# Two jobs per loop body over 18 weight slots, with jobs of 96 tokens, in the expert loop of a decoder layer

## The chip, the core and the metric

The kernel runs on one NeuronCore of one Trainium2 chip. The time is the device time of one execution in microseconds. In this text TensorE is PE in the rows, VectorE is DVE, ScalarE is ACT, GpSimd is POOL, and SyncE is SP; PEld is TensorE's weight load.

## The reference

One decoder layer over 512 tokens of width 1024, all in float32: an attention and pooling mixer, then a mixture of 32 experts of which each token takes four, then a last RMSNorm. The change touches the experts alone:

```python
def moe(h, router_w, router_b, w_gate_up, b_gate_up, w_down, b_down):
    logits = (h @ router_w + router_b).astype(jnp.float32)
    top_v, top_i = lax.top_k(logits, TOP_K)          # 4 of 32
    gates = jax.nn.softmax(top_v, axis=-1)
    ...
    def expert_block(args):
        xblk, e = args
        act = clamped_swiglu(xblk @ w_gate_up[e] + b_gate_up[e])
        return act @ w_down[e] + b_down[e]
```

An expert has 1024 x 2048 weights for gate and up and 1024 x 1024 for down, 12.6 MB together. 512 x 4 = 2048 (token, expert) pairs are spread over 32 experts, 64 each in the mean.

## The kernel before

The mixer and the router fill about the first 300 us. Then comes the expert loop, in jobs. A job is one expert with up to 128 of its tokens, cut into chunks of 32 (CH); it has as many chunks as its tokens need, and two at least (LEAST). An expert with more tokens than a job takes would get a second job. The job table (expert, first token, chunks, chunks before, gathered rows) is worked out by VectorE with one matmul (L625) and read by every engine into registers, once a job. With every expert in one job there are 32 jobs.

The weights of a job are 12 units of 1 MB: units 0 to 7 are gate and up (one for each 128 rows of the input), units 8 to 11 are down. The loop uses 12 of the 18 slots of 8 KB per partition that `ring` spans; slots 12 to 17 lie in memory that the mixer and the router use before. SyncE issues all weight loads in one queue, in order: for unit u of the next job it waits until TensorE has read the same unit of this one (`wait_read`), then issues. Unit 7 is released by `gu_done`, unit 11 by `dn_done`, the others by `units_used`, which the last chunk, chunk 0, counts up.

TensorE holds a chunk's 32 tokens as its weights and streams the expert's weights past it, four column tiles side by side. In a job it goes through units 0 to 3 with all chunks in turn, highest chunk first, then through units 4 to 7 for one chunk after another, then through the downs, one chunk after another. A chunk's down waits for its own activation (`act_done`), which VectorE and ScalarE work out (`swiglu`, `sigmoid`) in the order of the chunks while TensorE works on the next. There are code variants for four, three and two chunks:

```python
with pe.If(chunks > 2):
    with pe.If(chunks > 3):
        gates_together((3, 2, 1, 0))
        gate_rest(3)
    with pe.Else():
        gates_together((2, 1, 0))
    gate_rest(2)
with pe.Else():
    gates_together((1, 0))
```

Ahead of its gates, a job first does 16 small matmuls (`indices(job + 1)`, L619) that give the row indices of the next job's tokens. They wait for `hot_done` (VectorE, `job_columns`, L1090, late in the job before). VectorE copies the result (`job_rows`), GpSimd gathers the next job's rows with indirect DMAs (L920), VectorE flips them (`flip_x`, L1169, `x_done`). After a chunk's down VectorE adds the bias (`add_bias`, L1217, `y_done`) and GpSimd scatters the result (L941). The last scatter is followed by the combine: y_rows are read back (L377), summed with the router's gates (L1275), normed, and written.

Of the kernel before, what the change touches and what calls it, by code (L numbers as in the profile page):

```python
# [28 lines left out]
P = 128  # L29
# [23 lines left out]
NCH = P // CH  # L53
# [3 lines left out]
SLOTS = 12  # L57
# [10 lines left out]
JOBS_MAX = 49  # L68
# [16 lines left out]
C_END = C_AFTER + 49  # L85
# [12 lines left out]
def constants():  # L98
# [18 lines left out]
    n = np.arange(C_END - C_AFTER)[None, :]  # L117
    c[:, C_AFTER:C_END] = 16.0 * ((p[:, None] >= 1) & (p[:, None] <= n))
# [14 lines left out]
def program(nc, x, w_in, w_out, norm1, norm2, final_g, rel_bias, pool_w, pool_scale, router_w,  # L133
# [7 lines left out]
    with ExitStack() as ctx:  # L141
# [36 lines left out]
        job_r, job_p, keep_s = st[:, 44:48], st[:, 48:52], st[:, 52:56]  # L178
# [33 lines left out]
        jdiag = work[:, o + 1296:o + 1296 + ROWS * JOBS_MAX]  # L212
        jobs_f = sb("jobs_f", [P, ROWS, JOBS_MAX])
        jobs_i = sb("jobs_i", [P, ROWS, JOBS_MAX], I32)
        njobs_i = sb("njobs_i", [P, 1], I32)
# [9 lines left out]
        hot = work[:, 10240:11264].bitcast(F16).rearrange("p (t n) -> p t n", t=TT)  # L225
        slot = work[:, 11264:11520].bitcast(F16)
        pcol = work[:, 11520:11528].bitcast(F16)[:, 0:3 * TT].rearrange("p (t n) -> p t n", t=TT)
        idx_t = work[:, 11536:11544].rearrange("p (c n) -> p c n", c=NCH)
        idx_g = work[:, 11552:11556].bitcast(U32)
        idx_s = work[:, 11560:11564].bitcast(U32)  # L230
# [78 lines left out]
        def _(sp):  # L309
# [21 lines left out]
            def wait_read(job, u, low):  # L331
# [8 lines left out]
            def load_unit(e, u):  # L340
# [46 lines left out]
        def _(pe):  # L387
# [240 lines left out]
            def run_job(job, chunks, before_job, low):  # L628
# [56 lines left out]
                with pe.Else():  # L685
                    gates_together((1, 0))
# [651 lines left out]
```

## Time and profile before

| | |
|---|---|
| median of 3 runs | 1361.63 us (1360.19 to 1365.3) |
| the profiled execution | 1361.84 us, its span 1360.1 us |
| TensorE busy | 87% of the span, mean granted clock 0.938 |
| VectorE, ScalarE, GpSimd busy | 37%, 13%, 18% |
| DMA | 454.87 MB, 334 GB/s in the mean |
| chain that ended last | PE 67%, DMA 25%, VectorE 3%, issue 3% |

Times of events are in us from the start of the span. A profile row has a line number of the kernel before. "x192" counts records; a float32 matmul leaves two records, and its weight load two more. The idle time in brackets stands before the instruction, with what ended it. "issue" is a wait for nothing that the profile shows.

### The profile page before, as it was taken

What the parts mean: (1) busy time and instruction counts of PE and PEld (TensorE: products, weight loads), DVE (VectorE), ACT (ScalarE), POOL (GpSimd) and SP (SyncE); (2) the same over time, 40 slices, a digit from 0 to 9 for tenths busy, and PEclk for the clock granted to TensorE, in tenths of its full rate; (3) what the DMA queues carried; (4) which work ended last, traced back from release to release, by engine and by line L of the source; (5) the groups of instructions that cost most, each with busy time, mean ns of one, the idle gap of its engine ahead of it and who ended that gap; (6) DMA issues with size and microseconds to landing.
All of it is one profiled execution on the core that took longest, in us unless ns stands there. A gap on an engine that the chain in (4) does not pass through costs nothing.

```text
span 1360.1 us, 32747 instructions
## 1 busy us (share of the span) xinstructions
PE 1181.8 (87%) x11932; PEld 513.8 (38%) x11933; DVE 502.6 (37%) x1386; ACT 178.3 (13%) x328; POOL 245.2 (18%) x250
## 2 busy tenths in 40 slices
PE   6999998976999989999999997889998898878770
PEld 3674554551343333333333343223333233322220
DVE  2002332243453334444443353333443343433337
ACT  3013332210010101111111100001110010000002
POOL 0503433001112111111111111111112111111110
PEclk9999999986999999999999999889999899988885
DMA  9511210043899999999999999999999999999957
GB/s 378 225 62 63 77 67 12 32 155 142 361 420 419 420 419 419 419 419 418 408 389 399 419 420 420 420 418 419 420 421 418 420 419 421 420 420 420 420 232 308
DMA packets 71453, 454.87 MB, mean 334 GB/s; under 512 B 11013, under 2 KB 11325, under 8 KB 19974
## 3 DMA queue, kind: packets, MB, share of 16 engines
q1 hardware_dynamic: 61374, 430.49, 77.1%
q0 software_dynamic: 9360, 22.08, 4.3%
q10 hardware_dynamic: 696, 1.98, 0.5%
q8 instruction: 15, 0.25, 0.1%
q14 instruction: 8, 0.07, 0.0%
HBM read 444.37 MB, written 14.71 MB: 338 GB/s over the span
## 4 chain that ended last, share of the span: by engine, by line
PE 67%; DMA 25%; DVE 3%; issue 3%; ACT 1%; SPq 0%; DVEq 0%; POOLq 0%
PE bank L634 31%; PE bank L667 16%; DMA arena<-in_w_down 13%; DMA arena<-in_w_gate_up 11%; PE bank L424 8%; PE bank L494 4%; PE bank L440 3%; PE bank L453 1%; DVE xs L1275 1%; PE bank L481 1%; PE bank L467 1%; PE bank L619 1%; PE bank L398 1%; PE bank L573 1%; DMA xs<-in_x 0%
## 5 line engine op out<-in xcount | busy, mean ns | idle before, releaser
L634 PE MATMUL bank<-arena,hT 128*32 128x512 f32 x5120 | 602.9, 629 | 39.8 <-DMA arena<-in_w_gate_up 31.1
L634 PEld LDWEIGHTS bank<-arena,hT 128*32 128x32 f32 x5120 | 172.6, 115 | 443.9 <-issue 384.6
L667 PE MATMUL bank<-arena,hT 128*32 128x256 f32 x5120 | 289.0, 382 | 18.2 <-DMA arena<-in_w_down 18.1
L667 PEld LDWEIGHTS bank<-arena,hT 128*32 128x32 f32 x5120 | 167.4, 111 | 147.7 <-DMA arena<-in_w_down 27.2
L941 POOL DMA_INDIRECT y_rows<-hT,arena x80 | 80.4, 1005 | 655.3 <-DVE hT L1217 647.9
L1201 DVE TENSOR_TENSOR arena<-bank,gain 128x512 f32<-128x512 f32 x80 | 55.3, 692 | 347.9 <-PE bank L634 347.9
L828 ACT ACT_TABLE_LOAD x48 | 61.6, 1283 | 498.0 <-issue 497.7
L920 POOL DMA_INDIRECT hT<-h_rows,arena x83 | 84.6, 1019 | 201.1 <-issue 195.6
L424 PE MATMUL bank<-hT,arena 128*128 128x512 f32 x224 | 103.6, 610 | 0.8 <-ACT hT L726 0.8
L828 ACT ACTIVATE arena<-arena 128x256 f32<-128x256 f32 x80 | 33.3, 417 | 407.6 <-DVE arena L1203 407.6
L905 POOL TENSOR_SCALAR arena<-arena,st 128x128 f32<-128x128 f32 (+3 forms) x48 | 51.4, 1082 | 116.6 <-DVE st L1012 116.5
L1217 DVE TENSOR_TENSOR hT<-bank,gain 128x256 f32<-128x256 f32 x80 | 32.9, 423 | 89.3 <-PE bank L667 77.1
L494 PE MATMUL bank<-arena 128*128 128x512 f32 x128 | 59.2, 613 | 3.7 <-ACT arena L785 2.8
L619 PE MATMUL bank<-arena 128*128 128x3 f16 x528 | 18.3, 165 | 48.8 <-issue 42.2
L424 PEld LDWEIGHTS bank<-hT,arena 128*128 128x128 f32 x224 | 41.4, 192 | 50.2 <-issue 49.0
L1222 DVE LOAD_MASK_SELECT gain<-bias_row x32 | 0.4, 14 | 152.1 <-issue 152.1
L1031 DVE CUSTOM_DVE_ANT_0 arena<-bank,arena 128x128 f32<-128x128 f32 (+3 forms) x48 | 21.6, 488 | 69.7 <-PE bank L453 69.2
L1169 DVE STREAM_TRANSPOSE hT<-hT 128x256 f32<-128x256 f32 x83 | 46.7, 609 | 0.0
L440 PE MATMUL bank<-arena,hT 128*128 128x256 f32 x192 | 41.6, 379 | 0.0
L619 PEld LDWEIGHTS bank<-arena 128*128 128x128 f16 x528 | 15.4, 96 | 64.4 <-issue 56.9
L1090 DVE TENSOR_SCALAR arena<-arena,st 128x512 f16<-128x512 f16 x136 | 38.6, 348 | 0.0
L440 PEld LDWEIGHTS bank<-arena,hT 128*128 128x128 f32 x192 | 36.5, 190 | 5.4 <-issue 0.5
(138 smaller groups left out, 620.0 us busy)
## 6 DMA issues: line engine op xcount, KB each, us to landing
arena<-in_w_gate_up SPq DMA_DIRECT2D x256, 1024.0 KB, 20.9
arena<-in_w_down SPq DMA_DIRECT2D x128, 1024.0 KB, 22.0
arena<-in_w_in SPq DMA_DIRECT2D x10, 1024.0 KB, 18.1
arena<-y_rows SPq DMA_DIRECT2D x8, 1024.0 KB, 12.0
arena<-in_w_out SPq DMA_DIRECT2D x4, 1024.0 KB, 21.6
arena<-bias_by_dist POOLq DMA_DIRECT2D x6, 512.0 KB, 3.9
xs<-in_x SPq DMA_DIRECT2D x4, 512.0 KB, 6.9
h_rows<-arena POOLq DMA_DIRECT2D x4, 512.0 KB, 2.9
```

Of the source, the lines that this page charges most:

```text
L424: mm = pe.matmul(b[:, :], w[:, k, half * P:(half + 1) * P], hT[:, k, :], start=(k == 0), stop=(k == KT - 1))
L440: mm = pe.matmul(b[:, half * 256:(half + 1) * 256], hT[:, k, t * P:(t + 1) * P], w[:, k, :], start=(k == 0), stop=(k == KT - 1))
L494: mm = pe.matmul(b, mixT[:, k, t * P:(t + 1) * P], ring[:, s, c:c + 512], start=(k == 0), stop=(k == KT - 1))
L619: mm = pe.matmul(bank[7][:, 4 * c:4 * c + 3], hot[:, t, c * P:(c + 1) * P], pcol[:, t, :], start=(t == 0), stop=(t == TT - 1))
L634: mm = pe.matmul(bank[c][j * CH:(j + 1) * CH, :].rearrange("p (g n) -> p g n", g=2), xT[:, c, k * CH:(k + 1) * CH], w[:, :, j * Q:(j + 1) ...
L667: mm = pe.matmul(bank[c][j * CH:(j + 1) * CH, 0:Q], aT[:, c, k * CH:(k + 1) * CH], w[:, j * Q:(j + 1) * Q], start=(k == 0), stop=(k == KT ...
L828: act.activation(sg[:, c % 2, :], gu[:, c % 2, 0:Q], ACT.Sigmoid, scale=ALPHA)\
L905: pool.tensor_scalar(pv, pv, row_inv[:, h:h + 1], None, ALU.mult).then_inc(norm_done, 1)
L920: pool.indirect_dma_start(xg[:, c, :], None, h2_rows, bass.IndirectOffsetOnAxis(ap=idx_g[:, c:c + 1], axis=0), bounds_check=last_token, oo ...
L941: pool.indirect_dma_start(y_rows, bass.IndirectOffsetOnAxis(ap=idx_s[:, c:c + 1], axis=0), yb[:, c, :], None, bounds_check=last_row, oob_i ...
L1169: ins = dve.transpose(xT[:, c, :], xg[:, c, :].rearrange("p (i k) -> p k i", k=KT))
L1201: dve.tensor_tensor(gu[:, b, :], bank[c][:, :], bt[:, 0:2 * Q], ALU.add).then_inc(gu_read, 1)
```

## The change

A job has at most 96 tokens, three chunks. The loops of SyncE and TensorE have two jobs in their body. Units 0 to 5 of odd jobs lie in slots 12 to 17, those of even jobs in slots 0 to 5, and units 6 to 11 of all jobs share slots 6 to 11. After unit 11 of job 0, SyncE issues units 0 to 5 of job 1 into slots 12 to 17, the last two after the mixer's and router's last use of that memory (`ssq_done`, `tr_done`, `h2_out`). In the loop it then issues units 6 to 11 of a job and, behind them, units 0 to 5 of the next. Ahead of the loop it issues units 6 to 11 of job 1. The number of jobs is rounded up to an even one; the table's third row sums and limits come from constants.

TensorE has one code path for three and two chunks, with a branch around each of chunk 2's parts. The index matmuls, 12 instead of 16, stand after unit 3's gates. Chunk 2's down stands alone as before; the downs of chunks 1 and 0 go unit by unit, both after `act_done` of chunk 0. The other engines lose their parts for a fourth chunk.

Left out of the diff below: the constants (limits, triangle for the sums, even numbers), smaller tiles for three chunks, and the removed fourth chunk on ScalarE, GpSimd and VectorE.

```diff
@@ -50,11 +50,12 @@
 MASKED = -1e30
 
 CH = 32
-NCH = P // CH
+NCH = 3
+JT = NCH * CH
+BLOCKS = -(-S // JT)
 Q = D // 4
 UNIT = 2048
 RING = 18
-SLOTS = 12
...
 AHEAD = NCH - 1
-JOBS_MAX = 49
+HALF = 6
+JOBS_MAX = 56
...
@@ -328,7 +337,11 @@
                                      (pscale[:, :], pool_scale)):
                         sp.dma_start(dst, src).then_inc(small_in, 16)
 
-            def wait_read(job, u, low):
+            def ring_slot(half, u):
+
+                return u + JOB_UNITS if half and u < HALF else u
+
+            def wait_read(job, u, low=None):
 
                 if u == KT - 1:
                     sp.wait_ge(gu_done, low + AHEAD)
@@ -337,37 +350,55 @@
                 else:
                     sp.wait_ge(units_used, job * FREED + (u + 1 - (u >= KT)))
 
-            def load_unit(e, u):
+            def load_unit(e, u, half):
                 if u < KT:
                     src = w_gate_up[bass.ds(e, 1)].rearrange("e (p k) n -> (e k) p n", p=P)[u]
                 else:
                     src = w_down[bass.ds(e, 1)].rearrange("e (p u k) n -> (e u) p (k n)", p=P, k=2)[u - KT]
-                dst = ring[:, u, :]
-                sp.dma_start(dst, src).then_inc(unit_full[u], 16)
-
-            def load_job(e, job, low):
-
-                for u in range(JOB_UNITS):
-                    wait_read(job - 1, u, low)
+                sp.dma_start(ring[:, ring_slot(half, u), :], src).then_inc(unit_full[u], 16)
+
+            for n in range(KT):
+                sp.wait_ge(proj_done, 2 * (IN_UNITS - KT + n + 1))
+                load_unit(0, n, 0)
+            for n in (8, 9, 10):
+                sp.wait_ge(out_used, n - KT + 1)
+                load_unit(0, n, 0)
+            sp.wait_ge(op_done, TT)
+            load_unit(0, 11, 0)
+            for n in range(HALF):
+                if n == HALF - 2:
+                    sp.wait_ge(ssq_done, 2 * TT)
+                    sp.wait_ge(tr_done, 4 * TT)
+                    for b in range(2):
+                        sp.wait_ge(h2_out[b], 16 * TT // 2)
+                sp.wait_ge(unit_full[n], 16)
+                load_unit(1, n, 1)
+            sp.wait_ge(jobs_done, 2)
+
+            def load_part(e, job, half, units, low, free_of):
+
+                for u in units:
+                    wait_read(free_of, u, low)
                     sp.sem_inc(waited_sp, 1)
                     sp.wait_ge(unit_full[u], job * 16)
                     sp.sem_inc(waited_sp, 1)
-                    load_unit(e, u)
-
-            for n in range(KT):
-                sp.wait_ge(proj_done, 2 * (IN_UNITS - KT + n + 1))
-                load_unit(0, n)
-            for n in (8, 9, 10):
-                sp.wait_ge(out_used, n - KT + 1)
-                load_unit(0, n)
-            sp.wait_ge(op_done, TT)
-            load_unit(0, 11)
-            sp.wait_ge(jobs_done, 2)
-            njobs = sp.value_load(njobs_i[0:1, 0:1], min_val=E, max_val=JOBS_MAX - 2)
-            with sp.Fori(1, njobs) as job:
-                e = sp.value_load(jobs_i[0:1, 0, bass.ds(job, 1)], min_val=0, max_val=E - 1)
-                load_job(e, job, sp.value_load(jobs_i[0:1, 3, bass.ds(job, 1)], min_val=4, max_val=COUNT_MAX))
-            total = sp.value_load(jobs_i[0:1, 3, bass.ds(njobs, 1)], min_val=4, max_val=COUNT_MAX)
+                    load_unit(e, u, half)
+
+            def counted(job):
+
+                return sp.value_load(jobs_i[0:1, 3, bass.ds(job, 1)], min_val=4, max_val=COUNT_MAX)
+
+            load_part(1, 1, 1, range(HALF, JOB_UNITS), counted(1), 0)
+            more = sp.value_load(njobs_i[0:1, 2:3], min_val=E // 2 - 1, max_val=JOBS_MAX // 2 - 2)
+            with sp.Fori(0, more) as pair:
+                for half in range(2):
+                    job = pair * 2 + (2 + half)
+                    e = sp.value_load(jobs_i[0:1, 0, bass.ds(job, 1)], min_val=0, max_val=E - 1)
+                    low = counted(job)
+                    load_part(e, job, half, range(HALF), low, pair * 2 + half)
+                    load_part(e, job, half, range(HALF, JOB_UNITS), low, pair * 2 + (1 + half))
+            njobs = sp.value_load(njobs_i[0:1, 1:2], min_val=E, max_val=JOBS_MAX - 2)
+            total = counted(njobs)
             sp.wait_ge(scattered, total * 16)
             sp.sem_inc(waited_sp, 1)
             sp.wait_ge(dn_done, total + AHEAD)
@@ -625,11 +656,17 @@
             pe.matmul(bank[1][:, 0:ROWS * JOBS_MAX], ones, jdiag, start=True, stop=True).then_inc(jobs_mm, 1)
             pe.wait_ge(jobs_done, 2)
 
-            def run_job(job, chunks, before_job, low):
+            def run_job(job, half, chunks, before_job, low):
+
+                full = job * 16 + 16
+
+                def unit(u):
+
+                    return ring[:, u + JOB_UNITS if half and u < HALF else u, :]
 
                 def gate_step(c, k):
 
-                    w = ring[:, k, :].rearrange("p (g n) -> p g n", g=2)
+                    w = unit(k).rearrange("p (g n) -> p g n", g=2)
                     for j in range(4):
                         mm = pe.matmul(bank[c][j * CH:(j + 1) * CH, :].rearrange("p (g n) -> p g n", g=2),
                                        xT[:, c, k * CH:(k + 1) * CH], w[:, :, j * Q:(j + 1) * Q],
@@ -639,65 +676,62 @@
                     elif c == 0:
                         mm.then_inc(units_used, 1)
 
...
-
                 def gate_rest(c):
 
                     for k in range(KT // 2, KT):
                         if c > 0:
-                            pe.wait_ge(unit_full[k], job * 16 + 16)
+                            pe.wait_ge(unit_full[k], full)
                         gate_step(c, k)
 
...
+                def down_step(c, k):
+
+                    w = unit(KT + k // 2)[:, (k % 2) * D:(k % 2 + 1) * D]
+                    for j in range(4):
+                        mm = pe.matmul(bank[c][j * CH:(j + 1) * CH, 0:Q], aT[:, c, k * CH:(k + 1) * CH],
+                                       w[:, j * Q:(j + 1) * Q], start=(k == 0), stop=(k == KT - 1),
+                                       tile_position=(0, j * CH))
+                    if k == KT - 1:
+                        mm.then_inc(dn_done, 1)
+                    elif c == 0 and k % 2 == 1:
+                        mm.then_inc(units_used, 1)
+
+                pe.wait_ge(x_done, job + 1)
+                for k in range(KT // 2):
+                    pe.wait_ge(unit_full[k], full)
+                    if k == 0:
+                        pe.wait_ge(y_done, before_job + (AHEAD - 1))
+                    with pe.If(chunks > 2):
+                        gate_step(2, k)
+                    gate_step(1, k)
+                    if k == 0:
+                        pe.wait_ge(y_done, before_job + AHEAD)
+                    gate_step(0, k)
                 indices(job + 1)
-                pe.wait_ge(x_done, job + 1)
                 with pe.If(chunks > 2):
-                    with pe.If(chunks > 3):
-                        gates_together((3, 2, 1, 0))
-                        gate_rest(3)
-                    with pe.Else():
-                        gates_together((2, 1, 0))
                     gate_rest(2)
-                with pe.Else():
-                    gates_together((1, 0))
                 gate_rest(1)
                 gate_rest(0)
                 with pe.If(chunks > 2):
-                    with pe.If(chunks > 3):
-                        down(3, every)
-                    down(2, every)
-                down(1, every)
-                down(0, every)
-
-            njobs = pe.value_load(njobs_i[0:1, 0:1], min_val=E, max_val=JOBS_MAX - 2)
-            with pe.Fori(0, njobs) as job:
-                run_job(job, pe.value_load(jobs_i[0:1, 2, bass.ds(job, 1)], min_val=LEAST, max_val=NCH),
-                        pe.value_load(jobs_i[0:1, 3, bass.ds(job, 1)], min_val=2, max_val=COUNT_MAX),
-                        pe.value_load(jobs_i[0:1, 3, bass.ds(job + 1, 1)], min_val=4, max_val=COUNT_MAX))
+                    pe.wait_ge(act_done, low + (AHEAD - 2))
+                    for k in range(KT):
+                        if k % 2 == 0:
+                            pe.wait_ge(unit_full[KT + k // 2], full)
+                        down_step(2, k)
+                pe.wait_ge(act_done, low + AHEAD)
+                for k in range(KT):
+                    if k % 2 == 0:
+                        pe.wait_ge(unit_full[KT + k // 2], full)
+                    down_step(1, k)
+                    down_step(0, k)
+
+            pairs = pe.value_load(njobs_i[0:1, 0:1], min_val=E // 2, max_val=JOBS_MAX // 2 - 1)
+            with pe.Fori(0, pairs) as pair:
+                for half in range(2):
+                    job = pair * 2 + half
+                    run_job(job, half,
+                            pe.value_load(jobs_i[0:1, 2, bass.ds(job, 1)], min_val=LEAST, max_val=NCH),
+                            pe.value_load(jobs_i[0:1, 3, bass.ds(job, 1)], min_val=2, max_val=COUNT_MAX),
+                            pe.value_load(jobs_i[0:1, 3, bass.ds(job + 1, 1)], min_val=4, max_val=COUNT_MAX))
 
 
         @block.scalar
@@ -1128,9 +1156,10 @@
 
             dve.wait_ge(cnt_mm, 1)
             link(dve.tensor_copy(cnt, bank[1][:, 0:E]))
-            link(dve.tensor_scalar(nblk, cnt, float(P), None, ALU.is_gt))
-            for b in range(2, TT):
-                link(dve.scalar_tensor_tensor(nblk, cnt, float(b * P), nblk, ALU.is_gt, ALU.add))
...
...
-            link(dve.tensor_scalar(jcol[:, 5:6], jcol[:, 4:5], float(CH), 1.0, ALU.is_gt, ALU.add))
-            for c in range(2, NCH):
-                link(dve.scalar_tensor_tensor(jcol[:, 5:6], jcol[:, 4:5], float(c * CH), jcol[:, 5:6],
-                                              ALU.is_gt, ALU.add))
-            link(dve.tensor_scalar(jcol[:, 5:6], jcol[:, 5:6], float(LEAST), None, ALU.max))
-            before_j, after_j = tri_c[:, 0:JOBS_MAX], cst[:, C_AFTER:C_AFTER + JOBS_MAX]
+            link(dve.tensor_scalar(jcol[:, 5:6], jcol[:, 4:5], float(LEAST * CH), float(LEAST), ALU.is_gt, ALU.add))
...
             ins.then_inc(jdiag_done, 1)
+            pairs = jcol[:, 6:7]
+            link(dve.tensor_scalar(tmp32, cst[:, C_EVEN:C_EVEN + E], blk_end[:, E - 1:E], 0.0, ALU.is_lt, ALU.add,
+                                   accum_out=pairs))
+            dve.tensor_scalar(njobs_i[:, 2:3], pairs, 1.0, None, ALU.subtract)
+            dve.tensor_scalar(njobs_i[:, 1:2], pairs, 2.0, None, ALU.mult)
+            dve.tensor_copy(njobs_i[:, 0:1], pairs).then_inc(jobs_done, 1)
             dve.wait_ge(jobs_mm, 1)
             table = bank[1][:, 0:ROWS * JOBS_MAX].rearrange("p (r n) -> p r n", r=ROWS)
             link(dve.tensor_copy(jobs_f[:, :, :], table))
-            link(dve.tensor_scalar(jobs_f[:, 3, :], jobs_f[:, 3, :], 2.0, None, ALU.add))
-            dve.tensor_copy(njobs_i[:, :], blk_end[:, E - 1:E]).then_inc(jobs_done, 1)
             dve.tensor_copy(jobs_i[:, :, :], jobs_f[:, :, :]).then_inc(jobs_done, 1)
 
             gv = gates.rearrange("p (t k) -> p t k", t=TT)
```

## Rows read from the trace of the kernel before

**Rows 1.** Time slices of the page: GB/s in 40 slices of 34 us.
```profile
GB/s 378 225 62 63 77 67 12 32 155 142 361 420 419 420 419 419 419 419 418 408 389 399 419 420 420 420 418 419 420 421 418 420 419 421 420 420 420 420 232 308
```

**Rows 2.** Groups by line, all engines: busy us, mean ns | idle before.
```profile
L634 PE MATMUL bank<-arena,hT 128*32 128x512 f32 x5120 | 602.9, 629 | 39.8 <-DMA arena<-in_w_gate_up 31.1
...
L1210 DVE TENSOR_TENSOR gain<-arena 128x256 f32<-128x256 f32 x48 | 20.4, 425 | 1.6
```

**Rows 3.** Timeline of TensorE alone, jobs 2 and 3 and job 15: start, duration, instruction, count.
```profile
381.95 20.81 PE L634 MATMUL bank<-arena,hT 128*32 128x512 f32 x192 [0.20 <-issue]
...
402.57 10.55 PE L667 MATMUL bank<-arena,hT 128*32 128x256 f32 x192
...
414.60 0.55 PE L619 MATMUL bank<-arena 128*128 128x3 f16 x16 [1.49 <-issue]
...
415.28 15.64 PE L634 MATMUL bank<-arena,hT 128*32 128x512 f32 x128
...
430.73 7.09 PE L667 MATMUL bank<-arena,hT 128*32 128x256 f32 x128
...
798.55 13.94 PE L634 MATMUL bank<-arena,hT 128*32 128x512 f32 x128
```

**Rows 4.** Timeline of TensorE, matmuls that waited for the last units of a job.
```profile
494.30 6.15 PE L667 MATMUL bank<-arena,hT 128*32 128x256 f32 x80 [1.42 <-DMA arena<-in_w_down]
...
844.46 4.52 PE L667 MATMUL bank<-arena,hT 128*32 128x256 f32 x80 [1.42 <-DMA arena<-in_w_down]
...
1306.79 6.07 PE L634 MATMUL bank<-arena,hT 128*32 128x512 f32 x40 [1.22 <-DMA arena<-in_w_gate_up]
...
1316.58 4.52 PE L667 MATMUL bank<-arena,hT 128*32 128x256 f32 x80 [1.13 <-DMA arena<-in_w_down]
```

**Rows 5.** Timeline around the start of job 0, VectorE and TensorE.
```profile
313.31 0.28 DVE L1161 CAST jobs_i<-jobs_f 128x245 int32<-128x245 f32 x1
...
317.23 0.58 PE L619 MATMUL bank<-arena 128*128 128x3 f16 x16 [4.70 <-DVE arena L1090]
...
321.19 5.35 PE L634 MATMUL bank<-arena,hT 128*32 128x512 f32 x24 [3.38 <-issue]
...
321.19 23.66 PE L634 MATMUL bank<-arena,hT 128*32 128x512 f32 x192 [3.38 <-issue]
```

**Rows 6.** Instruction queue before 317 us and from 317 to 357, and work in 0 to 317.
```profile
q8 instruction: 9, 0.15, 0.2%
...
q8 instruction: 6, 0.10, 0.9%
...
0.00:317.00 317.00, 278.03 (x1180) 158.86 (x1181) 85.78 (x299) 76.34 (x187) 84.38 (x91) 0.95 0.31 116
```

**Rows 7.** Windows: busy us of each engine, clock, DMA share, GB/s.
```profile
325.00:330.00 5.00, 5.00 (x40) 1.25 (x36) 0.00 (x0) 1.28 (x1) 2.00 (x2) 0.80 0.45 137
...
325.00:360.00 35.00, 33.40 (x400) 12.41 (x396) 12.06 (x31) 3.81 (x5) 5.00 (x5) 0.94 0.79 309
```

**Rows 8.** Windows in which the DMA engines' share falls.
```profile
690.00:694.00 4.00, 4.00 (x52) 1.41 (x47) 3.12 (x7) 0.42 (x1) 0.00 (x0) 1.00 0.68 229
...
724.00:727.00 3.00, 3.00 (x40) 1.07 (x36) 2.26 (x7) 0.42 (x1) 0.00 (x0) 1.00 0.75 273
...
1303.00:1306.00 3.00, 1.14 (x12) 0.16 (x8) 0.00 (x0) 0.00 (x0) 0.00 (x0) 1.00 0.84 339
...
1312.00:1315.00 3.00, 3.00 (x54) 1.44 (x48) 1.88 (x5) 0.42 (x1) 0.00 (x0) 1.00 0.17 71
```

**Rows 9.** Timeline at the end of job 1's gates: TensorE and chunk 0's last activation step.
```profile
357.36 15.64 PE L634 MATMUL bank<-arena,hT 128*32 128x512 f32 x128 [0.16 <-issue]
...
375.31 0.66 DVE L1212 STREAM_TRANSPOSE hT<-gain 128x256 f32<-128x256 f32 x1
```

**Rows 10.** Timeline after the last matmul: last scatter, first transfer of the combine.
```profile
1322.42 1.00 POOL L941 DMA_INDIRECT y_rows<-hT,arena  x1 [1.13 <-DVE hT L1217]
...
1325.47 4.27 SPq L377 DMA_DIRECT2D arena<-y_rows  x8
```

More of the change, by code:

```diff
@@ L84 @@
 C_AFTER = 473
-C_END = C_AFTER + 49
+C_BEFORE = C_AFTER + 56
+C_LIMITS = C_BEFORE + 56
+C_EVEN = C_LIMITS + 5
+C_END = C_EVEN + 32
 ROWS = 5
@@ L640, in gate_step @@
                         mm.then_inc(units_used, 1)
-                def gates_together(chunk_list):
-                    for k in range(KT // 2):
-                        pe.wait_ge(unit_full[k], job * 16 + 16)
-                        for c in chunk_list:
-                            if k == 0:
-                                pe.wait_ge(y_done, before_job + (AHEAD - 1 if c else AHEAD))
-                            gate_step(c, k)
                 def gate_rest(c):
@@ L654, in gate_rest @@
                         if c > 0:
-                            pe.wait_ge(unit_full[k], job * 16 + 16)
+                            pe.wait_ge(unit_full[k], full)
                         gate_step(c, k)
-                def down(c, ks):
-                    pe.wait_ge(act_done, low + (AHEAD - c))
-                    for k in ks:
-                        u = KT + k // 2
-                        if c > 0 and k % 2 == 0:
-                            pe.wait_ge(unit_full[u], job * 16 + 16)
-                        w = ring[:, u, (k % 2) * D:(k % 2 + 1) * D]
-                        for j in range(4):
-                            mm = pe.matmul(bank[c][j * CH:(j + 1) * CH, 0:Q], aT[:, c, k * CH:(k + 1) * CH],
-                                           w[:, j * Q:(j + 1) * Q], start=(k == 0), stop=(k == KT - 1),
-                                           tile_position=(0, j * CH))
-                        if k == KT - 1:
-                            mm.then_inc(dn_done, 1)
-                        elif c == 0 and k % 2 == 1:
-                            mm.then_inc(units_used, 1)
@@ L675, in run_job @@
-                every = range(KT)
+                def down_step(c, k):
[8 more added lines that the diff above has]
+                        mm.then_inc(units_used, 1)
@@ L819, in _ @@
             act.wait_ge(jobs_done, 2)
[L820 removed]
+            njobs = act.value_load(njobs_i[0:1, 1:2], min_val=E, max_val=JOBS_MAX - 2)
             with act.Fori(0, njobs) as job:
@@ L833, in _ @@
                 with act.If(chunks > 2):
-                    with act.If(chunks > 3):
-                        sigmoid(3)
                     sigmoid(2)
@@ L948, in _ @@
                 with pool.If(next_chunks > 2):
-                    with pool.If(next_chunks > 3):
-                        gather(3, gathered)
                     gather(2, gathered)
@@ L954, in _ @@
                 with pool.If(chunks > 2):
-                    with pool.If(chunks > 3):
-                        scatter(3)
                     scatter(2)
@@ L1226, in _ @@
                 with dve.If(chunks > 2):
-                    with dve.If(chunks > 3):
-                        swiglu(3)
                     swiglu(2)
@@ L1235, in _ @@
                 with dve.If(next_chunks > 2):
-                    with dve.If(next_chunks > 3):
-                        flip_x(3, False)
                     flip_x(2, False)
@@ L1247, in _ @@
                 with dve.If(chunks > 2):
-                    with dve.If(chunks > 3):
-                        add_bias(3)
                     add_bias(2)
```

38 lines of the change are left out of this document (23 added, 15 removed).

## The prediction

> **What bounds the kernel now.** I read the time slices of the page first [rows 1]. For the first 300 us the DMA engines carry little, and then the expert loop keeps them at 418 to 421 GB/s almost to the end: 384 weight units of 1.05 MB, 403 MB, of 455 MB in all. TensorE is busy in 87% of the span, so the groups by line come next [rows 2]. A chunk has 8 x 4 gate matmuls of two records each, so 5120 records are 80 chunks. The 48 products written to gain are those of chunks 0 and 2, so with 32 jobs 16 have a chunk 2; the other 80 - 48 = 32 are the chunks 1, and none is left for a chunk 3. So no expert has more than 96 tokens, 16 jobs have three chunks and 16 have two. In order of time the three-chunk ones are jobs 0, 2, 4, 6 to 12, 14, 19 to 21, 24 and 26 (by their record counts of 192 and 128).
>
> TensorE's timeline gives the price of a job [rows 3]: three chunks 20.8 + 10.4 us, two chunks 15.6 + 6.9 us (a down's row begins 0.2 before the gates' row ends) (13.9 where the clock stays up), and 2.1 us from the last down to the next gate, of which 0.55 are the index matmuls. A three-chunk job is 33.3 us, a two-chunk job 23 to 25. Against this stands the stream. The places where a down waits for unit 11 of a job give its pace [rows 4]: job 5 at 494.30, job 16 at 844.46, job 31 at 1316.58, so 31.8 and 31.5 us a job. Before 812 us TensorE is mostly the slower of the two, since ten of sixteen jobs have three chunks; from job 16 on the stream is, and it ends the loop. What counts is when the stream starts, whether it is ever held up, and what follows its last unit.
>
> **The start of job 0.** Today the job table is cast at 313.59, TensorE reads registers until 317.23, does the index matmuls of job 1, and then stands 3.38 us for nothing that a row names, until 321.19 [rows 5]. In 317 to 357 us six packets of the instruction queue come in, after nine in the 317 us before, and none follow; 15 packets are 0.25 MB, 16 KB each [rows 6]. So I read the 3.38 us as a jump to code not yet fetched: a three-chunk job skips the four-chunk variant. The change has no such variant, so I take that stall at zero (bounds 0 and 3.4). The index matmuls no longer stand ahead (-0.6), and the table is about 0.6 us earlier (three comparisons for the blocks become two operations, four for the chunks become one, the addition behind the table's copy goes, and the pair count is worked out under the table's matmul; an estimate from operations of 0.15 to 0.3 us like the cast). Three flips instead of four make x ready at about 315, before TensorE's registers are. Job 0 then starts at 321.2 - 3.4 - 0.6 - 0.6 = 316.6 (316.0 to 321.2).
>
> **The stream's start.** 325 to 360 us carried 309 GB/s x 35 = 10.8 MB, 25.8 us at 419 GB/s [rows 7]: the stream runs as if it had begun at 334.2. After: units 12 to 17 go out from 290 us on. They are 6.3 MB, 15 us, in slices that now carry 155 and 142 GB/s [rows 1], so they are done by 310, and the gathers of 307 to 312 us meet only their tail (I cost that at 0, at most 3 us on job 0). Then SyncE stands at unit 6 of job 1, which waits for job 0's use of the same slot, and units 0 to 5 of job 2 stand behind it in the queue. Gates end 23.7 + 0.5 after the start, at 340.8, and unit 6 is free at 339.9. The lag from free to moving is 1.9 us (24 records end at 326.5; 137 GB/s in 325 to 330 is 1.6 us of traffic, so it began at 328.4 [rows 5, 7]). Unit 8 is free after chunk 2's downs and two paired steps, 340.8 + 3.45 + 1.73 = 346.0, and moves at 347.9. From there the stream is full, with eight units more than job 0's twelve landed: 347.9 - 8 x 2.62 = 326.9. Gain 7.3 us; with the start of job 0 unmoved 2.7. This is less than half of the 15.7 us that six units are worth, since the stream stands idle from 310 to 342, where today it begins at 328.
>
> **Held up later.** Today it idles when its 12 slots are full, about 4 us in 690 to 694 and 724 to 727 [rows 8]. I cost the removal of that at nothing: jobs 6 to 16 took 31.8 us each against 31.5 later, and with nine of eleven three-chunk jobs against five of fifteen, each chunk moving 0.26 MB, 0.3 us of this is traffic. The reason is in the last slices: the engines' share falls from 0.84 to 0.17 between 1303 and 1315 while the last unit lands at 1316.58 [rows 4, 8]. Some engines trail, the units wait for those, and the idle ones are the others. Bounds: -5 to 0. The other way, a stream 7 us earlier meets TensorE no earlier in jobs 11 and 12: the six slots allow 15.7 us more lead, of which 7.3 and the 4 idle ones are used up, and I add 1.4 us (0 to 4).
>
> **Two-chunk jobs.** Downs of chunks 1 and 0 now start together, so they wait for chunk 0's activation. Gates end at 373.00 and it is ready at 375.97 [rows 3, 9]: 3.0 us that chunk 1's downs (3.45) hide now. Three chunks hide it under chunk 2's, with 0.5 us to spare. TensorE gains 4.6 at the start and about 0.4 a job from the moved index matmuls (0.55 less 12 of 16 of it, and a loop end in every second job only), and pays 3.0 in jobs 1, 3, 5, 13, 15 and 16. By the end of job 16 it stands at 849.4 by my sum, today at 848.98; by job 18 it waits for the stream again. So this costs nothing there, since two-chunk jobs of 26 to 28 us are still faster than 31.5. If it brings a clock drop each time (1.7 us: 15.64 against 13.9) the catch-up is one job later. The order of index matmuls makes DVE's job_rows and POOL's gathers some 10 us later in the job; they have that long before flip_x.
>
> **The tail.** Unit 7 of job 31 lands at 1306.79, gates end 6.07 later at 1312.86, the activation of chunk 0 is there at 1315.83, and 6.9 us of downs end at 1322.7, where chunk 1's early start lets them end at 1321.10 today [rows 4, 9]: +1.6. Both add_bias and both scatters then follow the end; today only chunk 0's does (scatter at 1322.42, next transfer at 1325.47 [rows 10]). That is one more POOL issue of 1.0 + 0.3, less 0.2 because chunk 1 ends that much earlier: +1.1. "Unit by unit" would win only if unit 11 came more than 8 us after the gates. Tail +2.7, from 0.5 (the gates of job 31 without the clock drop that makes their 40 records 6.07 instead of 4.3 us, and the downs then end with today's) to 3.
>
> **Sum.** 1361.84 (the profiled run's own time; median of the runs 1361.63) - 7.3 + 1.4 + 2.7 = 1358.6.
>
> **Rivals.** (A) The sum, 1352 to 1364: chance 0.44. (B) The idle 4 us counts and the lead is kept, and the tail costs only 0.5: 1361.8 - 7.3 - 4 + 0.5 = 1351: 0.14. For it: DVE and the slots do get free; against: the pace above. (C) Job 0 does not start earlier, or the gathers are late under the new traffic: -2.7 + 1.4 + 2.7 = 1363.2: 0.12. (D) Slower: the loop's code no longer stays. 2361 records in 317 us came with nine packets, some 262 a packet [rows 6]. The body today is 336 + 16 matmuls, 1376 records and some 45 control steps, 5.4 packets, and is not fetched again. The new one has 2 x (192 x 4 + 24) = 1584 and my estimate of 70 to 110 control steps, 6.4 packets, which with its two ends touches eight. If that is one too many, each return of the loop pays a stall like the 3.38. Eight returns before job 16 are 27 us of a TensorE that is just then the slower one, and the stream's spare lead of 4 takes little: by job 12 it is held 20 - 4 = 16, by job 16 some 18 to 22. 1358.6 + 18 = 1377. It decides from the point where the loop needs one packet more than the chip keeps: 0.25. If the refetches also slow one of the DMA engines, it is dearer still: 0.05.
>
> [...]
>
> **Numbers.** The forecast is A's 1358.6. The range goes from 1350.5, which holds about half of B, to 1379, which leaves out D's upper third and the dearer 0.05; together some 0.2. A alone is 1352 to 1364. Within 0.5% (6.8 us, what these runs can tell from nothing) lies 1354.8 to 1368.4: most of A, all of C. Faster: B and a fifth of A, 0.23. Slower: D and a few clock drops, 0.30. Same 0.47.
>
> **What the profile after would show.** Instruction packets: none in the loop for A, some in every pair of jobs for D, with 3 us of issue before every second job. The first gate record of job 0 at 316 to 317. GB/s near 0 from 310 to 341, full from 348. Waits of 3 us on DVE before the downs of two-chunk jobs. Units landing 6 us earlier from job 18 to 31. The last scatter 2.4 us after the last matmul. I am wrong if TensorE falls behind the stream after job 18, or if trailing DMA engines catch up in the idle 30 us and keep it.

## The result, and the profile after

The changed kernel takes 1454.39 us (median of 4 runs, 1446.26 to 1459.45) beside 1360.91 for the kernel before on the same chip: ratio 1.067, 95% interval 1.065 to 1.070. 1358.6 was predicted, in a range of 1350.5 to 1379.

The page of the changed kernel: slices, the instruction queue, the chain, and the three groups of TensorE that matter.
```profile
PEclk9999999969897989898989898989998898979895
...
GB/s 381 185 69 66 58 68 1 121 235 234 418 359 419 327 418 354 382 327 396 306 402 301 419 349 417 416 410 399 318 399 373 417 353 417 357 418 401 417 162 292
...
q8 instruction: 151, 2.47, 0.7%
...
PE 80%; issue 10%; DVE 8%; DMA 1%; ACT 1%; DVEq 0%; SPq 0%; POOLq 0%; POOL 0%
...
L671 PE MATMUL bank<-arena,hT 128*32 128x512 f32 x5120 | 600.5, 622 | 141.0 <-issue 121.5
...
L690 PE MATMUL bank<-arena,hT 128*32 128x256 f32 x5120 | 305.3, 401 | 48.0 <-DVE hT L1241 48.0
```
The slices of [rows 1] that stood at 420 GB/s now swing between 300 and 419. The chain holds 1% of DMA: TensorE, its issue and VectorE carry the loop. The instruction queue has 151 packets where there were 15, and the gates have 121.5 us of "issue" before them where [rows 2] has 39.8 us of idle time in all, mostly waits for units.

TensorE's timeline in the changed kernel, jobs 1 to 4; in brackets the idle time before.
```profile
370.81 8.40 PE L690 MATMUL bank<-arena,hT 128*32 128x256 f32 x128 [3.00 <-DVE hT L1241]
386.73 12.37 PE L671 MATMUL bank<-arena,hT 128*32 128x512 f32 x96 [7.52 <-issue]
...
399.42 10.51 PE L671 MATMUL bank<-arena,hT 128*32 128x512 f32 x96
409.75 10.54 PE L690 MATMUL bank<-arena,hT 128*32 128x256 f32 x192
421.82 7.07 PE L671 MATMUL bank<-arena,hT 128*32 128x512 f32 x64 [1.53 <-issue]
...
439.29 9.99 PE L690 MATMUL bank<-arena,hT 128*32 128x256 f32 x128 [3.00 <-DVE hT L1241]
457.00 3.64 PE L671 MATMUL bank<-arena,hT 128*32 128x512 f32 x16 [7.73 <-issue]
```
Its instruction queue in windows: 317 to 385 us, and from 385 us to the end.
```profile
q8 instruction: 8, 0.13, 0.8%
...
q8 instruction: 134, 2.20, 0.8%
```
Between the two jobs of a body TensorE idles 1.1 to 1.5 us, at each return of the loop 7.4 to 8.2 (15 returns, 115.4 us together). The first half of the gates after a return takes 12.4 us, the second half, as many matmuls of the same kind, 10.51. In the first 4 us the granted clock is 0.52, in 395.1 to 399.1 us it is 1.00. The first of the two:
```profile
386.70:390.70 4.00, 3.97 (x20) 1.15 (x24) 0.00 (x0) 1.28 (x1) 0.00 (x0) 0.52 1.01 416
```
Nine packets come per return: 9 x 15 = 135 of the 151 (378 to 448, 448 to 518 and 880 to 944 us each hold nine). Two come in 377 to 387 us, about TensorE's idle time ahead of the first gate. Elsewhere a packet comes in ahead of its use: one in 346 to 349 us and one in 402 to 405 us, with TensorE busy in 3.00 of the 3 us in both. Every two-chunk job waits 3.00 us for its activation.

### The profile page after: what moved, and what is told of

Read it like the earlier page. It is cut to its first block, busy times and chain, and to the rows that moved or that the text cites. A ratio compares the mean times of both kernels' runs of the same rounds, so it can differ in the third digit from the quotient of the medians.

```text
span 1455.7 us, 32162 instructions
## 1 busy us (share of the span) xinstructions
PE 1192.7 (82%) x11800; PEld 515.7 (35%) x11801; DVE 502.7 (35%) x1383; ACT 178.3 (12%) x328; POOL 244.3 (17%) x249
## 4 chain that ended last, share of the span: by engine, by line
PE 80%; issue 10%; DVE 8%; DMA 1%; ACT 1%; DVEq 0%; SPq 0%; POOLq 0%; POOL 0%
PE bank L671 41%; PE bank L690 20%; PE bank L455 7%; PE bank L525 4%; PE bank L471 3%; DVE hT L1246 2%; PE bank L484 1%; DVE xs L1298 1%; PE bank L512 1%; PE bank L650 1%; PE bank L498 1%; DVE arena L1230 1%; DVE hT L1241 1%; PE bank L429 1%; PE bank L604 0%
## 5 line engine op out<-in xcount | busy, mean ns | idle before, releaser
L671 PE MATMUL bank<-arena,hT 128*32 128x512 f32 x5120 | 600.5, 622 | 141.0 <-issue 121.5
L671 PEld LDWEIGHTS bank<-arena,hT 128*32 128x32 f32 x5120 | 173.2, 114 | 526.6 <-issue 521.2
L690 PE MATMUL bank<-arena,hT 128*32 128x256 f32 x5120 | 305.3, 401 | 48.0 <-DVE hT L1241 48.0
L690 PEld LDWEIGHTS bank<-arena,hT 128*32 128x32 f32 x5120 | 171.2, 116 | 192.7 <-DVE hT L1241 62.5
L1125 DVE COPY st<-bank 128x3 f32<-128x3 f32 x33 | 5.3, 161 | 274.1 <-PE bank L650 274.1
L1236 DVE SCALAR_TENSOR_TENSOR arena<-arena 128x256 f32<-128x256 f32 x80 | 34.0, 425 | 8.5
L1050 DVE COPY arena<-bank 128x128 f32<-128x128 f32 (+3 forms) x24 | 11.8, 490 | 72.5 <-PE bank L498 72.5
```

Source lines behind the costliest of these rows:

```text
L671: mm = pe.matmul(bank[c][j * CH:(j + 1) * CH, :].rearrange("p (g n) -> p g n", g=2), xT[:, c, k * CH:(k + 1) * CH], w[:, :, j * Q:(j + 1) ...
L690: mm = pe.matmul(bank[c][j * CH:(j + 1) * CH, 0:Q], aT[:, c, k * CH:(k + 1) * CH], w[:, j * Q:(j + 1) * Q], start=(k == 0), stop=(k == KT ...
```

## The experiments

Three readings of the 93 us stood against each other. **F**: the loop's code no longer stays and is fetched anew each time (rival D of the prediction). **W**: the new order of the downs or of the index matmuls. **S**: slots and early loads, that is traffic. F is tested by waits that are long fulfilled, put ahead of TensorE's loop, which shift the loop's code and do nothing in it. The experiments ran on several chips, on which the kernel before took 1361.5 to 1364.1 us; each ratio is to the kernel before on its own chip. Where no ratio is given the time is that of one run.
```
             pe.sem_inc(dn_done, 2 + AHEAD)
+            for _ in range(N):
+                pe.wait_ge(dn_done, 1)
```

**N = 144.** 

> The changed kernel with 144 more instructions on TensorE, waits that are already met, ahead of its first matmul, where TensorE stands idle for 8.9 us anyway. They shift the loop's code by a bit over half a 16 KB packet; the loop itself is unchanged, word for word. Theory F (the loop with its two ends and the look-ahead needs nine packets, one more than the chip keeps, so each pair of jobs fetches all of them again): after the shift the same code touches one packet less, it stays, the instruction queue shows some 15 to 18 packets in all instead of 151, the 7.6 us of issue before every second job fall to under 2, and the time is 1350 to 1365 us. Theory W (the 7.6 us are a wait of the new order, chunk 1's and chunk 0's biases coming late, or register reads): nothing changes, 1450 to 1460 us, idle 7.6 us at every second job.

Measured: 1356.62 us (6 runs), ratio 0.9947 (0.9931 to 0.9964): 98 us less than the changed kernel, and faster than the kernel before (1364.04 on that chip). Its page, and its timeline at the return to job 2, where the changed kernel idles 7.52 us and needs 12.37 for the same gates:
```profile
GB/s 377 229 62 47 93 48 32 32 254 104 351 419 419 420 420 418 420 418 417 403 405 396 420 419 420 421 419 419 420 420 419 421 417 420 420 420 420 421 193 308
...
q8 instruction: 16, 0.26, 0.1%
...
PE 70%; DMA 20%; DVE 6%; issue 3%; ACT 1%; POOL 0%; SPq 0%; DVEq 0%; POOLq 0%
...
L673 PE MATMUL bank<-arena,hT 128*32 128x512 f32 x5120 | 572.4, 599 | 71.1 <-issue 30.8
...
L692 PE MATMUL bank<-arena,hT 128*32 128x256 f32 x5120 | 304.4, 399 | 48.8 <-DVE hT L1243 48.0
```
```profile
371.26 8.51 PE L692 MATMUL bank<-arena,hT 128*32 128x256 f32 x128 [3.00 <-DVE hT L1243]
381.50 10.51 PE L673 MATMUL bank<-arena,hT 128*32 128x512 f32 x96 [1.72 <-issue]
```
Nothing that the loop executes has changed, its 3.0 us waits included. F is shown; W and S are not the cause of the loss.

**N = 40.** 

> The same with 40 waits instead of 144, a control. Theory F: the shift is too small to bring the loop's start over the next packet border (it begins some 117 instructions before one), so it stays at nine packets a pair and about 1450 to 1460 us, some 150 instruction packets. If any added wait helped, or theory W with some luck of timing, it would be near e1's time.

Measured: 1463.68 us (3.7 over what was stated), 151 packets. Waits ahead of the loop are no cure in themselves. The place of the border in this expectation was wrong, as is shown below.

**300 waits in the four-chunk variant of the kernel before, which no job enters.** 

> The kernel before, with 300 waits added inside the four-chunk branch of its TensorE loop, which no job takes: dead code that only makes the loop's body longer (1424 + 300 instructions) and is jumped over. Theory F: from its start at 0.57 of a packet the body now touches eight packets and a ninth is looked ahead, so it is fetched again at each of the 32 jobs: over 200 instruction packets, a stall of 3 to 8 us a job, 1361 + 100 to 250 us. Theory W: dead code costs nothing, 1361 us.

Measured: 1362.61 us, 15 packets. The expectation missed, but this run doesn't tell whether code that is jumped over counts. Two waits are one instruction (see below), so 150 were added and not 300. In the trace this loop starts at record 2,446; with 1424 + 150 instructions it ends near 4,020, ahead of the border at 2,493 + 6 x 256 = 4,029 that follows from the runs below. By that count it lies in the same seven packets as without them, if only by some ten instructions. The added code does take up room: from 317 to 330 us the kernel before fetches two packets and this one three, and from 317 to 357 us both fetch six. This run from 317 to 330 us:
```profile
q8 instruction: 3, 0.05, 1.4%
```

**The change without the two-job body, the slots and the early loads** (96-token jobs, index matmuls mid-job, paired downs, 12 slots). 

> The changed kernel with one job per loop body and 12 slots as before, no units ahead: what is left of the change is jobs of 96 tokens, the index matmuls in mid-job and the last downs unit by unit. Theory F: no refetch (body some 830 instructions), so near the kernel before: job 0 starts 2 to 4 us earlier, but the 3 us waits for the activation in two-chunk jobs and the tail of 2.7 us come: 1358 to 1366 us. If the order of the matmuls itself were the cost, over 1400 us.

Measured: 1361.94 us (10 runs), ratio 0.9982 (0.9968 to 0.9995), 12 packets; the time is as stated.

Four parts were then taken back one at a time, each with N = 144, so with a loop that stays. Twelve slots:
```
-                return u + JOB_UNITS if half and u < HALF else u
+                return u
...
-                load_unit(1, n, 1)
```


> The changed kernel with the 144 waits ahead of the loop, and with 12 slots and no early loads in place of 18 (jobs of 96 tokens and two jobs per loop body stay). If the six slots are what makes the fitting kernel faster than the one before (0.9947), this one is like the one-job body with 96-token jobs: ratio 0.997 to 1.000, about 1361. If two jobs per body do it by themselves, it stays at 0.994 to 0.996, about 1357. Instruction queue in both cases 15 to 17 packets; if it has over 100, what makes the loop refetch is not cured by the 144 waits but hangs on something else.

Downs chunk by chunk:
```
-                for k in range(KT):
-                    if k % 2 == 0:
-                        pe.wait_ge(unit_full[KT + k // 2], full)
-                    down_step(1, k)
-                    down_step(0, k)
+                for c in (1, 0):
+                    pe.wait_ge(act_done, low + (AHEAD - c))
+                    for k in range(KT):
+                        if c and k % 2 == 0:
+                            pe.wait_ge(unit_full[KT + k // 2], full)
+                        down_step(c, k)
```


> The changed kernel with the 144 waits, and with the downs of chunk 1 ahead of those of chunk 0 as in the kernel before, in place of both chunks unit by unit. Theory: the waits of 3.0 us on the last activation are hidden behind the transfers in all jobs but the last, so only the last one counts: 3.0 us less wait, but chunk 0 ends 3.5 us after chunk 1 as before; 1 to 3 us faster than the 1356.6 of the fitting kernel, 1354 to 1356, ratio 0.992 to 0.994. Rival: the transfers' end decides and the wait costs nothing in the last job either, 1356 to 1358. Second rival: what the wait costs in every two-chunk job delays the freeing of slots, and the whole gains 5 us or more, under 1352.

Units 12 to 17 issued behind the wait for the jobs:
```
             load_unit(0, 11, 0)
+            sp.wait_ge(jobs_done, 2)
             for n in range(HALF):
...
-            sp.wait_ge(jobs_done, 2)
```


> The changed kernel with the 144 waits, and with the loads of units 12 to 17 issued after the jobs are known in place of before. 18 slots stay. If the early loads fill the time in which the transfers stood still, they give 6 units of 5.05 us at most and less what is late at the end: time 2 to 8 us longer than 1356.6, so 1358.5 to 1364. If it was the place to hold more that counted, and not the earlier start, nothing moves: 1356 to 1358.

Index matmuls ahead of the gates:
```
+                indices(job + 1)
                 pe.wait_ge(x_done, job + 1)
...
-                indices(job + 1)
```


> The changed kernel with the 144 waits, and with the index matmuls of the next job ahead of the gates as before, in place of mid-job. Theory: their 0.5 us stood ahead of each job's first gates, but from the fourth job on the transfers bound the kernel, so only job 0 counts: 0 to 1 us longer than the fitting kernel, 1356.5 to 1358. Rival: what waits behind them (the gather of the next job's rows) starts earlier and the next job's first gates no longer wait, so faster, under 1356.

Measured against the kernel before, each with its interval: 12 slots 0.9972 (0.9960 to 0.9985), separate downs 0.9950 (0.9934 to 0.9966), no early loads 0.9974 (0.9962 to 0.9987), index matmuls first 0.9946 (0.9931 to 0.9961). All have 16 packets; the medians are 1359.33, 1355.50, 1357.62 and 1355.26 us, beside 1361.47 for the kernel before. So the slots without the early loads give nothing, and with them about 0.25%, some 3.5 us: the two kernels without early loads lie at 0.9972 and 0.9974, those with them at 0.9944 to 0.9950 (that of the next run included), though the intervals of single pairs just touch. The order of the downs and the place of the index matmuls give nothing that was measured, the 3.0 us waits included: separate downs missed the 0.992 to 0.994 stated for them, the index matmuls first were not slower, and without early loads the median is 0.9 us under the 1358.5 stated, though its ratio is in line with it. Two jobs per body alone give nothing clear either (0.9972 with 12 slots beside 0.9982 for one job per body).

**Separate downs and index matmuls first together, N = 144.** 

> The kernel with the 144 waits, the downs chunk by chunk (as in the sixth run) and the index matmuls ahead of the gates (as in the eighth), so that of the change the slots, the early loads, the jobs of 96 tokens and the two jobs per body are left. Both undone parts made no measurable difference alone, 0.9950 and 0.9946 beside 0.9947. If they are worth nothing together either, 0.994 to 0.996, about 1356; if each hid the other's gain, under 0.993, below 1353.

Measured: 1354.75 us, ratio 0.9944 (0.9930 to 0.9958), the lowest of the timed kernels, and not apart from 0.9947.

**12 slots, no waits ahead of the loop.** 

> The changed kernel with 12 slots and no early loads, and without waits ahead of the loop. The refetching hangs on TensorE's code alone, so 151 packets. Time: if the idle at each return and the slower gates hold TensorE up whether or not there are slots to load into, as in the changed kernel, 1452 to 1460. If the six more slots soften it by letting transfers run on during the idle, this one is longer, 1465 to 1500.

Measured: 1450.01 us, 151 packets. TensorE's code alone decides; six more slots don't soften it.

**Separate downs, no waits ahead of the loop.** 

> The changed kernel without waits ahead of the loop, so refetching, with the downs chunk by chunk as in the kernel before. If TensorE is the bound in the changed kernel, the wait of 3.0 us ahead of the downs of its 16 jobs of two chunks, which cost nothing in the fitting kernel (0.9950 beside 0.9947), counts here in full: 3.0 us less wait and up to 0.9 us shorter downs in each, 16 x 3.0 to 3.9 = 48 to 62 us, so 1392 to 1406 us, with 151 packets still. Rival: the refetching alone sets the time, and the wait is hidden as in the fitting kernel: 1450 to 1460 us.

Measured: 1404.57 us, 151 packets. Job 1's downs and the return behind them:
```profile
367.76 7.09 PE L690 MATMUL bank<-arena,hT 128*32 128x256 f32 x128
382.53 12.81 PE L671 MATMUL bank<-arena,hT 128*32 128x512 f32 x96 [7.68 <-issue]
```
The return is as dear as before, the wait is gone, and 50 us with it: 16 jobs by 3.0. What is worth nothing in the fitting loop is worth all of its length here, as TensorE has become the bound.

**Where the border lies.** Four runs were made on it. All four were stated with a border that was wrong, and with each wait counted as an instruction.

> The changed kernel with 72 waits that are long fulfilled ahead of the loop, where 144 cured the refetching and 40 did not. Theory by packets of 256 instructions: TensorE asks for a new packet near its instruction record 2,500 (at 2,480 in the changed kernel, at 2,500 with 40 waits), so the loop starts at 2,443 ahead of that border, at 2,483 just ahead of it, and with 72 waits at 2,515 behind it: it touches one packet less, 7 with one looked ahead to, and stays. About 1357 us and 15 to 17 packets. Rival: the cure needs more than one border, or was a matter of an alignment that 144 hit by chance: about 1455 us and 151 packets.

> The changed kernel with 232 waits ahead of the loop. Theory by packets: a pair of jobs of three chunks is 1,636 records, so the loop ends at 2,443 + 232 + 1,636 = 4,311, behind the border at about 2,490 + 7 x 256 = 4,282, and touches one packet more again: refetching as in the changed kernel, 151 packets, about 1455 us. Rival: any shift of more than 60 instructions cures it, because only the start of the loop counts: about 1357 us and 15 to 17 packets.

> The changed kernel with 112 waits ahead of the loop. In the run with 72 waits the loop start (record 2,515) was followed by a second stall after one matmul, some 25 records on: the packet border lies there, near record 2,540, and not near 2,490 as taken before. The start must lie behind it: 2,443 + N > 2,540, so N over 97. With 112 the loop starts at 2,555, touches 7 packets and stays: about 1357 us, 15 to 17 packets. Rival (the border is elsewhere between 72 and 144, or not what counts): about 1455 to 1490 us and 151 packets.

> The changed kernel with 272 waits ahead of the loop, which is 16 and one packet of 256. If the packets count, the loop lies in them as with 16 waits: its end, at 2,443 + 272 + 1,636 = 4,351, is behind the border at 2,540 + 7 x 256 = 4,332, it touches 8 packets and refetches: 151 to 153 packets, 1450 to 1490 us. Rival: any shift of over 100 cures it: about 1357 us and 15 to 18 packets.

Measured: 72 waits 1487.82 us, 232 waits 1357.34, 112 waits 1354.17, 272 waits 1362.97, and 16 packets in all but the first, which has 151. So 72, 232 and 272 missed, and 112 came out as stated by luck. With 72 the loop start is just ahead of a border, and ten of the 15 returns stall twice, the second time after one matmul; the other five idle once, 10.6 to 11.8 us:
```profile
385.20 1.05 PE L673 MATMUL bank<-arena,hT 128*32 128x512 f32 x1 [7.56 <-issue]
388.20 12.62 PE L673 MATMUL bank<-arena,hT 128*32 128x512 f32 x95 [1.95 <-issue]
```
The misses had a plain reason in the traces: line 422 shows 71 records for 144 waits and 135 for 272, so two waits are one instruction and N shifts by N / 2. (144 waits were thus 72 instructions, over a quarter of a packet and not over half as stated.) By that the unshifted start, at record 2,438, moves to 2,474 with 72 waits (the second stall comes about 20 records on) and 2,494 with 112, so the border is about 2,493, and the next ones are taken as 256 apart, an estimate beside the 262 records a packet of [rows 6]. Two runs were stated with this:

> The changed kernel with 400 waits ahead of the loop. The traces show one instruction for two of these waits (71 records for 144, 135 for 272), so 400 shift the loop by 200 instructions. With the border near record 2,494 and one every 256, a pair of 1,636 and an unshifted start at 2,438, the start is behind one border (2,638) and the end at 4,274 just ahead of the one at 4,286: 7 packets touched, no refetching, about 1357 to 1363 us and 16 or 17 packets. If the borders are off by more than 12 instructions it refetches.

> The changed kernel with 512 waits ahead of the loop, 256 instructions by two waits each, one whole packet. If it is the place in the packets that decides, the loop lies as in the changed kernel without waits and refetches: about 151 packets and 1450 to 1462 us. Rival: any shift of 56 instructions or more cures it: 1357 to 1365 us and 16 to 18 packets.

Measured: 400 waits 1368.65 us and 16 packets, 512 waits (one whole packet) 1474.59 us and 152. The packets are as stated, so a shift by 256 instructions puts the loop where it was, and the times are longer: 400 took 5.7 us more than the 1363 given, 512 12.6 more than the 1462. The waits also hold up the front: job 0 starts at 318.94 with 144, at 328.30 with 400 and at 335.78 with 512.

## Why the prediction was wrong

**The step that failed** is the instruction fetch at the loop's return. The sum of 1358.6 has it at nothing, as it takes the loop's code to stay, and where the prediction gave it a price, in rival D, the price was too small: "each return of the loop pays a stall like the 3.38", counted for eight returns, "by job 16 some 18 to 22", and with it D's 1377. D's condition came true: "one packet more than the chip keeps". No row before shows that eight touched packets are one too many; it was D's estimate, and these runs show it. The loop's 1,636 records (52 of control, where D estimated 70 to 110) touch eight packets of 256 with its two ends, as was counted. Then nine come in at each return (151 packets in the run), and not one alone; the ninth, more than the loop touches, fits a packet that is looked ahead to. With N = 112 to 400 the records touch seven packets, and none comes after 385 us (16 packets in the run).

The term measured 98 us (1454.4 against 1356.6; spans 1455.7 and 1358.0). Windows from 317 to 1420 us of the changed kernel and of N = 144, with the same matmuls:
```profile
317.00:1420.00 1103.00, 912.98 (x10624) 356.12 (x10624) 392.68 (x1061) 94.90 (x128) 160.89 (x159) 0.91 0.91 366
```
```profile
317.00:1420.00 1103.00, 884.03 (x10624) 345.05 (x10624) 418.61 (x1093) 101.97 (x141) 160.91 (x159) 0.96 0.91 373
```
- Idle time at the return: 7.69 us in the mean instead of 1.74, 15 times: 89 us, where D had 27. The prediction took the 3.38 us ahead of job 0, one jump, as the price; why a return that fetches costs 6 us more than one that doesn't is not shown.
- A lower clock: 913.0 - 884.0 = 29 us more busy time in the same matmuls (granted 0.91 against 0.96). Gates behind an idle stretch run slower: 0.52 granted in 386.70 to 390.70, and 12.37 us instead of 10.51 for the same matmuls. D had nothing for it.
- Against these, the waits for units go, some 20 us of idle time at the gates: 141.0 - 121.5 = 19.5 us is not issue, beside 71.1 - 30.8 = 40.3 in N = 144. 89 + 29 - 20 = 98.
- D stopped counting at job 16, where the stream takes over in [rows 4]. With some 8 us more in each pair, TensorE is the slower one to the end (the chain that ended last has 1% of DMA), and little is absorbed. The 3.0 us of the two-chunk jobs, "costs nothing", become 50 of these 1454 us: true only while the stream has the lead.

**The chance.** D had 0.25 and its dearer form 0.05, since no row before shows how many packets stay. By these runs a loop over seven packets of 256 stays (16 packets in all with N = 112, 144, 232, 272 and 400), and one over eight does not (151 or 152 with none, N = 40, 72 and 512).

**The sum of A, on the kernel whose loop stays.** It gave 1361.84 - 3.2. N = 144 measured 7 us less than the kernel before (0.9931 to 0.9964, so 5 to 9), its profiled run 2.1 less in span.
- The stall at job 0: right that it goes (none of 3.38 behind the index matmuls), but job 0 starts at 318.39 in the changed kernel, not 316.6. The cast of the job table starts at 314.31 (314.80 with N = 144) where [rows 5] has 313.31, so the table is 1.0 to 1.5 us later in these traces, and nothing came of the 0.6 that it should have been earlier.
- The stream's start: near nothing to 342 us and full behind it, as predicted. In N = 144:
```profile
318.00:342.00 24.00, 23.06 (x204) 6.85 (x208) 7.19 (x19) 3.40 (x4) 2.00 (x2) 0.90 0.04 11
342.00:350.00 8.00, 8.00 (x152) 4.81 (x148) 5.69 (x17) 0.42 (x1) 0.55 (x1) 1.00 0.87 310
```
- The end, N = 144: unit 7 of job 31 and the last downs.
```profile
1301.92 4.50 PE L673 MATMUL bank<-arena,hT 128*32 128x512 f32 x40 [1.38 <-DMA arena<-in_w_gate_up]
...
1309.42 8.77 PE L692 MATMUL bank<-arena,hT 128*32 128x256 f32 x128 [3.00 <-DVE hT L1243]
```
The unit is 4.9 us earlier than in [rows 4] (7.3 - 1.4 = 5.9 predicted), the first transfer of the combine, at 1322.99, 2.5 us earlier than in [rows 10]: the tail costs 2.4 (2.7 predicted). That the early loads gain is borne out by their removal (0.9974 against 0.9947). Why the medians differ by 5 to 9 us and the sum by 3.2 is not settled; the traces of these two executions, 2.1 apart, are nearer to the sum.
- The dips of the stream (slices 20 to 22 of N = 144, at 403, 405 and 396 GB/s) are still there with 18 slots: nothing from the slots alone, as costed.
- Of C only the smaller half is seen: job 0 starts 2.8 us earlier where A had 4.6, and the gathers were not late.

## What to carry to other kernels

Before a loop body is doubled, count the instructions of the whole body, branches not taken included, and find where it starts: divide by the packet's instructions (taken as 256 here), and count the packets that it touches with both ends. On TensorE here seven stayed (16 packets in the run) and eight did not (151). Branches not taken count: the return at 888.69 us, to two jobs of two chunks, brought nine packets like the others. If the count is one over, price it as all packets fetched anew at every return (nine, and 7.69 us of idle time in the mean, here), with the slower gates behind the idle time (12.37 us instead of 10.51, 0.52 granted in their first 4 us), and re-price all that was hidden while another engine was the bound. A few instructions ahead of the loop can move it to fit: here 56 to 200 of them (112 to 400 waits) were worth 86 to 100 us. Each of them also delays the front: with 400 waits job 0 starts 9.4 us later than with 144.

## What the runs showed of the hardware

- The refetching is periodic in the code's place: shifts of 0, 20 and 36 instructions refetch (1454, 1464, 1488 us), 56, 72, 116, 136 and 200 don't (1354 to 1369), 256 does again (1475).
- Nine packets come in at each return where the loop touches eight (151 in the run), none where it touches seven (16). A loop start just ahead of a border is the worst case seen, 1488 us, with a second stall of 1.5 to 2.1 us at ten of 15 returns.
- Code that is jumped over takes up packets (with 150 instructions more in a branch not taken, three packets come from 317 to 330 us instead of two). Whether enough of it would bring refetching was not tested: with these 150 the loop needs no packet more (1362.6 us, 15 packets).
- A return of the loop whose code stays costs 1.7 us of TensorE's idle time ahead of the next gates, one that fetches 7.4 to 8.2 us in the changed kernel.
